# A four-layer decoder trunk on one core: a new opening, whole tiles from GpSimd, and another order at the norms and in the attention mixer

## The chip, the cores and the metric

The kernel runs on one core of a Trainium2 chip. The metric is the device time of one execution in microseconds (us). TensorE is called PE here (PEld is its weight load), VectorE DVE, ScalarE ACT, GpSimd POOL, and SyncE SP.

## The reference

Two layers (the depth of this case), each with a half-step SwiGLU feed-forward network (FFN), a token mixer and another half-step FFN; the mixer of layer 0 is an mLSTM (mixer A), that of layer 1 differential attention (mixer B). Sequence 512, model width 1024, FFN width 2816, all in fp32.

```python
for i in range(DEPTH):
    ada = (cond @ ada_w[i] + ada_b[i]).reshape(-1, 3, 3, D_MODEL)
    h = modulate(x, norm_g[i, 0], ada[:, 0, 0], ada[:, 0, 1])   # rmsnorm(x, g) * (1 + scale) + shift
    x = x + 0.5 * ada[:, 0, 2, None, :] * swiglu(h, ffn_w13[i, 0], ffn_w2[i, 0])
    h = modulate(x, norm_g[i, 1], ada[:, 1, 0], ada[:, 1, 1])
    y = mlstm_mixer(h, ...) if i % 2 == 0 else diff_attn_mixer(h, ...)
    x = x + ada[:, 1, 2, None, :] * y
    h = modulate(x, norm_g[i, 2], ada[:, 2, 0], ada[:, 2, 1])
    x = x + 0.5 * ada[:, 2, 2, None, :] * swiglu(h, ffn_w13[i, 1], ffn_w2[i, 1])
return rmsnorm(x, final_g)
```

## The kernel before, in words

**Data and products.** x is kept transposed, as 8 tiles (k = 0 to 7) of 128 features by 512 tokens. Each fp32 product is made of three matmuls of rounded parts, hi x hi, lo x hi and hi x lo (`three`, L710 to L712). Weights come in units of 128 x 1024, eight blocks of 128 x 128, one per k: SP loads a unit into one of two buffers (`load_unit`, L545; the load of unit u waits until the low part of unit u - 2 is made), ACT makes its high part (L1212), DVE its low part (L1707), and PE needs both. With 512 tokens a unit is 8 products, 24 matmuls. Each engine works through its own written list of instructions in order, and semaphores join them; so what stands behind a waiting instruction on its engine waits too.

**Norms.** Five norms stand between the six sublayers, and one at the end; n = 1, 3 and 4 follow an FFN, n = 2 and 5 a mixer. Each works in two halves of 256 tokens. Per k DVE makes the modulated tile (L1767), ACT the high part h_hi, with the shift as bias (L1220, the "split"), and DVE h_lo = tile + shift - h_hi (L1719, the "low"). For k = 2, 4 and 6 of half 0, ACT adds the shift to the tile in place (L1225) and POOL makes h_lo from it (L698), a "joint". Between these stand the high and low parts of the first units U to U + 3 of the next sublayer. PE's `first_group` begins on the tiles as they come: in half 0 units 0 and 1 side by side, k by k, then units 2 and 3; in half 1 units 0 to 2 side by side, then unit 3.

**FFN.** An FFN p (0 to 3; after norms 0, 2, 3 and 5) has 8 plain pairs of gate and up units in p = 0 and 4 in the others, then 14 or 18 fast pairs, which need fewer products, of sums of tiles. These sums (L1869 on DVE, split on ACT at L1283, and their low parts) are made from whole modulated tiles `mod`, the shift included; ACT makes them (`full_modulated`, L1275). The low parts of the first factors of weights (L1914) come behind them. The gate products are ACT's L1261 (from PSUM) and DVE's L1849, g_lo is L1854. Before the fast pairs SP writes x into DRAM (`store_x`, L571), since its space is used.

**Opening.** For FFN 0 the modulation vectors of norm 0 are made on DVE (L1812, one pass for scale and one for shift per k) from eight slices `early_ada` of 1 MB. For k = 4 to 7 POOL makes the shift's product (L693) and ACT sums it. Per k DVE makes the tile `mod` (L2446) and h_lo (L2451), and ACT columns of scale and shift and h_hi (L1658). ACT also keeps half of x's tiles (`keep_x`, L1635). POOL makes the low parts of units 0 to 3 (L685). PE's `opening_group` (L806) works on units 0 to 3, with matmuls on zeros (L821) put in: 8 before the first product and 24 between the products.

**Mixer B.** DVE's loop over passes n does, per pass: mask and maxima of the scores (L2304 to L2306), a rotation of one head's q or k (`rope`, L2293 to L2297), a low part and copies of head outputs. PE makes scores (L1096) and column sums (`head_sum`, L1132).

## Time and profile before

| | |
|---|---|
| time, median of 3 runs (lowest, highest) | 1906.97 us (1905.39, 1909.76) |
| the profiled execution: its time, its span | 1905.79 us, 1903.9 us |
| PE busy | 1867.1 us, 98% of the span |
| DVE, ACT, POOL busy | 1430.1 us (75%), 894.9 us (47%), 35.9 us (2%) |
| mean granted PE clock | 0.996 |
| chain that ended last | PE 82%, DVE 9%, ACT 3%, DMA 3%, issue 2% |
| DMA | 273.51 MB, mean 144 GB/s |

The span is that of one execution recorded by the profiler. A busy engine is one with an instruction in work. The granted clock is what the throttle allows PE, as a share of 2.4 GHz. A wait is idle time of an engine in front of an instruction, put down to the instruction that released it.

### The profile page before, as it was taken

Reading aid. Unit: us, or ns where it says so; the run is one execution under the profiler, and the core shown is the slowest. Engines: PE = TensorE matmul, PEld = TensorE weight load, DVE = VectorE, ACT = ScalarE, POOL = GpSimd, SP = SyncE. Lnnn points to the kernel's source line nnn. Section 1 sums busy time; section 2 is a strip of 40 time slices with the busy share of each in tenths; the row PEclk is TensorE's granted clock in tenths of the full one; section 3 lists DMA queues with packets and bytes.
Section 4 is the critical chain, followed back from the end, with each engine's and each line's share of the span. In section 5 each row is a group of like instructions: output and inputs, shape, how many; then the busy total and the mean of one; then the engine's idle time right before and its main releaser. Section 6 shows DMA issues by size and latency. Waiting matters only on the chain.

```text
span 1903.9 us, 30428 instructions
## 1 busy us (share of the span) xinstructions
PE 1867.1 (98%) x11752; PEld 1678.9 (88%) x11752; DVE 1430.1 (75%) x2000; ACT 894.9 (47%) x1435; POOL 35.9 (2%) x35
## 2 busy tenths in 40 slices
PE   7999999999999999999999999999999999999997
PEld 5799998888778999998899999889877799999886
DVE  6788868686577888868678888796786778888434
ACT  6266542244344656642265565224444456566321
POOL 4000000000000000000000000000000000000000
PEclk9999999999999999999999999999999999999999
DMA  8733259624213432349733322973321233323432
GB/s 345 265 111 111 100 183 338 240 89 155 66 56 101 133 111 90 109 179 334 260 122 122 110 89 86 344 254 89 111 67 45 67 124 121 109 90 105 135 98 82
DMA packets 86002, 273.51 MB, mean 144 GB/s; under 512 B 8560, under 2 KB 18928, under 8 KB 84888
## 3 DMA queue, kind: packets, MB, share of 16 engines
q1 hardware_dynamic: 85712, 271.83, 41.6%
q8 instruction: 51, 0.84, 0.2%
q10 hardware_dynamic: 200, 0.52, 0.1%
q14 instruction: 39, 0.32, 0.0%
HBM read 261.82 MB, written 10.50 MB: 143 GB/s over the span
## 4 chain that ended last, share of the span: by engine, by line
PE 82%; DVE 9%; ACT 3%; DMA 3%; issue 2%; SPq 0%; DVEq 0%; ACTq 0%
PE outp L711 12%; PE outp L712 12%; PE outp L710 12%; PE acc L710 11%; PE acc L712 11%; PE acc L711 11%; PE stats L710 2%; PE stats L712 2%; PE stats L711 2%; DVE w_lo L1707 2%; DMA arena<-w 1%; PE outp L1000 1%; DMA early_ada<-ada 1%; ACT w_hi L1212 1%; ACT mod L1275 1%
## 5 line engine op out<-in xcount | busy, mean ns | idle before, releaser
L710 PE MATMUL acc<-h_hi,w_hi 128*128 128x256 f32 (+1 forms) x1220 | 397.8, 326 | 11.1 <-DVE w_lo L1707 5.5
L1212 ACT ACTIVATE w_hi<-arena 128x1024 fp32r<-128x1024 f32 (+2 forms) x231 | 209.9, 909 | 383.4 <-DMA arena<-w 192.5
L711 PE MATMUL acc<-h_lo,w_hi 128*128 128x256 f32 (+1 forms) x1220 | 389.2, 319 | 0.0
L712 PE MATMUL acc<-h_hi,w_lo 128*128 128x256 f32 (+1 forms) x1220 | 389.1, 319 | 0.0
L1914 DVE TENSOR_TENSOR w_lo<-arena,w_hi 128x1024 fp32r<-128x1024 f32 (+1 forms) x272 | 290.5, 1089 | 101.7 <-ACT w_hi L1292 97.9
L1707 DVE TENSOR_TENSOR w_lo<-arena,w_hi 128x1024 fp32r<-128x1024 f32 (+2 forms) x229 | 236.6, 1035 | 165.6 <-ACT w_hi L1212 164.2
L1292 ACT ACTIVATE w_hi<-arena 128x1024 fp32r<-128x1024 f32 (+1 forms) x272 | 257.8, 949 | 75.8 <-PE stats L712 28.6
L710 PE MATMUL outp<-g_hi,w_hi 128*128 128x512 f32 (+1 forms) x792 | 290.2, 366 | 0.0
L711 PE MATMUL outp<-g_lo,w_hi 128*128 128x512 f32 (+1 forms) x792 | 289.5, 365 | 0.0
L712 PE MATMUL outp<-g_hi,w_lo 128*128 128x512 f32 (+1 forms) x792 | 289.4, 365 | 0.0
L710 PEld LDWEIGHTS acc<-h_hi,w_hi 128*128 128x128 f32 x1220 | 232.6, 191 | 34.8 <-issue 9.8
L711 PEld LDWEIGHTS acc<-h_lo,w_hi 128*128 128x128 f32 x1220 | 232.8, 191 | 17.3 <-issue 1.4
L712 PEld LDWEIGHTS acc<-h_hi,w_lo 128*128 128x128 f32 x1220 | 232.6, 191 | 16.5
L710 PEld LDWEIGHTS outp<-g_hi,w_hi 128*128 128x128 f32 x792 | 149.4, 189 | 24.4
L711 PEld LDWEIGHTS outp<-g_lo,w_hi 128*128 128x128 f32 x792 | 149.4, 189 | 24.3
L712 PEld LDWEIGHTS outp<-g_hi,w_lo 128*128 128x128 f32 x792 | 149.3, 189 | 23.7
L710 PE MATMUL acc<-t_hi,w_hi 128*128 128x256 f32 x544 | 154.0, 283 | 0.0
L711 PE MATMUL acc<-t_lo,w_hi 128*128 128x256 f32 x544 | 154.0, 283 | 0.0
L712 PE MATMUL acc<-t_hi,w_lo 128*128 128x256 f32 x544 | 154.0, 283 | 0.0
L710 PE MATMUL outp<-h_hi,w_hi 128*128 128x256 f32 x436 | 123.8, 284 | 0.0
L712 PE MATMUL outp<-h_hi,w_lo 128*128 128x256 f32 x436 | 123.4, 283 | 0.0
L711 PE MATMUL outp<-h_lo,w_hi 128*128 128x256 f32 x436 | 123.4, 283 | 0.0
(280 smaller groups left out, 3426.7 us busy)
## 6 DMA issues: line engine op xcount, KB each, us to landing
arena<-w SPq DMA_DIRECT2D x174, 512.0 KB, 3.7
ada_raw<-ada SPq DMA_DIRECT2D x64, 512.0 KB, 5.9
arena<-ada SPq DMA_DIRECT2D x56, 512.0 KB, 5.9
arena<-w SPq DMA_DIRECT2D x64, 384.0 KB, 3.6
arena<-w SPq DMA_DIRECT2D x64, 320.0 KB, 4.5
arena<-wa SPq DMA_DIRECT2D x33, 512.0 KB, 3.6
arena<-wb SPq DMA_DIRECT2D x32, 512.0 KB, 3.6
early_ada<-ada SPq DMA_DIRECT2D x8, 1024.0 KB, 17.7
```

Source lines behind the costliest of these rows:

```text
L710: pe.matmul(bank, a_hi, b_hi, start=start, stop=False, skip_group_check=onto)
L711: pe.matmul(bank, a_hi, b_lo, start=False, stop=False, skip_group_check=onto)
L712: return pe.matmul(bank, a_lo, b_hi, start=False, stop=stop, skip_group_check=onto)
L1000: last = pe.matmul(outp[:, d, j * P:S], a_v[:, j, c0:c0 + P], w, start=j == 0, stop=j == ST - 1)
L1212: act.activation(w_hi[base % SLOTS][:, 0:n], src[:, 0:n], ACT.Copy).then_inc(hi_ready, 1)
L1275: act.activation(mod[:, k, t], mod[:, k, t], ACT.Identity, bias=ada_v[:, 3 * N_FFN[p], k:k + 1]).then_inc(full_ready, 1)
L1292: act.activation(slot(w_hi[(B + n) % SLOTS], n), two_factors(j, n), ACT.Copy).then_inc(hi_ready, 1)
L1707: dve.tensor_tensor(w_lo[s][:, 0:n], raw[base % RAWS][:, 0:n], w_hi[s][:, 0:n].bitcast(F32), ALU.subtract).then_inc(lo_ready, 1)
L1914: dve.tensor_tensor(slot(w_lo[s], n), two_factors(j, n), slot(w_hi[s], n).bitcast(F32), ALU.subtract)\
```

## The change

- **Opening.** The modulated tile of each k goes to the PSUM bank `stat` instead of `mod`, one buffer for all k. DVE makes low(0) ahead of the passes of k = 1, and later each low between the scale pass and the shift pass of the next k. ACT makes the split of k = 0 before it keeps x tiles 6 and 7, and its high parts 1 to 3 stand at other places. PE's zero matmuls start when two x tiles are kept on ACT, go to bank 1, and are 8 + 12; the order of the products of k = 0 and 1 is another. SP writes x to DRAM behind the first early slices and before the load of unit 6. In FFN 0's first pair ACT's high part of unit 4 stands before the gate.
- **Norms.** There are no joints; DVE makes all h_lo. For n = 1, 3 and 4 ACT's high part of U + 2 stands behind the split of k = 0, for n = 2 and 5 behind that of k = 4; that of U + 3 stands behind all splits of half 0. For n = 2 and 5 DVE's low part of U + 1 stands before `add(4)`. In half 1 PE takes units 0 to 2 side by side for k < 6 alone, and then k = 6 and 7 unit by unit.
- **Whole tiles.** POOL makes them, as h_hi + h_lo (32 instructions of 512 columns, 8 per FFN); ACT's 32 are gone. In FFN 0 each follows its low, in the others all follow the last low of the norm.
- **Mixer B.** The rotations of passes 6 and 10 stand ahead of the maxima.

The places where the order of instructions changes, as lists of one engine. **ACT at the head of norm 1** (`w_hi_54` to `w_hi_57` hold the high parts of units U to U + 3). Before:

```order
L1229 ACTIVATE rstd<-stats,eps 128x256 [waits stat_done]
L1212 ACTIVATE w_hi_54<-arena 128x1024 [waits unit_done,raw_loaded0]
L1212 ACTIVATE w_hi_55<-arena 128x1024 [waits unit_done,raw_loaded1,ada_ready]
L1220 ACTIVATE h_hi<-mod,ada_v 128x256 [waits src_ready] x3
L1225 ACTIVATE mod<-mod,ada_v 128x256
L1220 ACTIVATE h_hi<-mod,ada_v 128x256 [waits src_ready] x2
L1225 ACTIVATE mod<-mod,ada_v 128x256
L1212 ACTIVATE w_hi_56<-arena 128x1024 [waits unit_done,raw_loaded0]
L1220 ACTIVATE h_hi<-mod,ada_v 128x256 [waits src_ready] x2
L1225 ACTIVATE mod<-mod,ada_v 128x256
L1212 ACTIVATE w_hi_57<-arena 128x1024 [waits unit_done,raw_loaded1]
L1220 ACTIVATE h_hi<-mod,ada_v 128x256 [waits src_ready]
```

And now, where line numbers are lower:

```order
L1225 ACTIVATE rstd<-stats,eps 128x256 [waits stat_done]
L1211 ACTIVATE w_hi_54<-arena 128x1024 [waits unit_done,raw_loaded0]
L1211 ACTIVATE w_hi_55<-arena 128x1024 [waits unit_done,raw_loaded1,ada_ready]
L1219 ACTIVATE h_hi<-mod,ada_v 128x256 [waits src_ready]
L1211 ACTIVATE w_hi_56<-arena 128x1024 [waits unit_done,raw_loaded0]
L1219 ACTIVATE h_hi<-mod,ada_v 128x256 [waits src_ready] x7
L1211 ACTIVATE w_hi_57<-arena 128x1024 [waits unit_done,raw_loaded1]
```

Unit U + 2 moved from behind the fifth split to behind the first, seven splits stand behind it, and the activations of `mod` are gone.

**DVE in the opening**, from the first tile on (`ISA` on early_ada is a pass). Before:

```order
L2446 SCALAR_TENSOR_TENSOR mod<-x,scale_col,stats 128x512 [waits rstd_spread,scale_made]
L1812 ISA early_ada,early_sum<-early_ada,outp 128x1024 [waits early_loaded1]
L1812 ISA early_sum 128x1
L1812 ISA early_ada,early_sum<-early_ada,outp 128x1024
L1812 ISA early_sum 128x1
L2451 SCALAR_TENSOR_TENSOR h_lo<-mod,ada_v,h_hi 128x512 [waits act_hi_ready]
L2446 SCALAR_TENSOR_TENSOR mod<-x,scale_col,stats 128x512 [waits scale_made]
```

And now:

```order
L2445 SCALAR_TENSOR_TENSOR stats<-x,scale_col,stats 128x512 [waits rstd_spread,scale_made]
L2450 SCALAR_TENSOR_TENSOR h_lo<-stats,ada_v,h_hi 128x512 [waits act_hi_ready]
L1805 ISA early_ada,early_sum<-early_ada,outp 128x1024 [waits early_loaded1]
L1805 ISA early_sum 128x1
L1805 ISA early_ada,early_sum<-early_ada,outp 128x1024
L1805 ISA early_sum 128x1
L2445 SCALAR_TENSOR_TENSOR stats<-x,scale_col,stats 128x512 [waits act_lo_ready,scale_made]
```

The low of k = 0 moved ahead of both passes of k = 1; each later tile waits for the low before it, since it has the same buffer.

**DVE in pass 6 of mixer B**, maxima and rotation. Before:

```order
L2304 TENSOR_TENSOR acc<-acc,mask_ts 128x2x128 [waits s_done]
L2305 TENSOR_REDUCE row_max<-acc 128x2 [waits dve_step]
L2306 TENSOR_SCALAR neg_max<-row_max 128x2 [waits dve_step]
L2293 STREAM_SHUFFLE b_rot<-b_qk 32x512 [waits acc_free0]
L2294 TENSOR_TENSOR b_tmp<-b_qk,b_cos 32x512 [waits dve_step]
L2296 TENSOR_TENSOR b_rot<-b_rot,b_sin 32x512
L2297 TENSOR_TENSOR b_qk<-b_tmp,b_rot 32x512 [waits dve_step]
L1707 TENSOR_TENSOR w_lo_61<-arena,w_hi_57 128x1024 [waits hi_ready,rope_done]
```

And now:

```order
L2286 STREAM_SHUFFLE b_rot<-b_qk 32x512 [waits acc_free0]
L2287 TENSOR_TENSOR b_tmp<-b_qk,b_cos 32x512 [waits dve_step]
L2289 TENSOR_TENSOR b_rot<-b_rot,b_sin 32x512
L2290 TENSOR_TENSOR b_qk<-b_tmp,b_rot 32x512 [waits dve_step]
L2297 TENSOR_TENSOR acc<-acc,mask_ts 128x2x128 [waits s_done,rope_done]
L2298 TENSOR_REDUCE row_max<-acc 128x2 [waits dve_step]
L2299 TENSOR_SCALAR neg_max<-row_max 128x2 [waits dve_step]
L1700 TENSOR_TENSOR w_lo_61<-arena,w_hi_57 128x1024 [waits hi_ready]
```

The four instructions of the rotation moved ahead of the three of the maxima.

The diff, without the lines in which `lows_made` becomes a plain wait:

```diff
@@ -142,11 +142,2 @@
 Q_IN = (Q_F0, Q_A, Q_F1, Q_F2, Q_B, Q_F3, Q_RESULT)
-POOL_LOWS = tuple(Q_IN[n] + k for n in range(1, SUBS) for k in (2, 4, 6))
-def pool_lows(i):
-    return sum(t < i for t in POOL_LOWS)
 HALVES = tuple(SQ_BASE[r] - KT * r for r in range(SUBS))
@@ -569,3 +551,7 @@
-                    sp.wait_ge(src_ready, Q_IN[n] + KT * (half + 1 if p else 1))
+                    if p:
+                        sp.wait_ge(src_ready, Q_IN[n] + KT * (half + 1))
+                    else:
+                        sp.wait_ge(x_kept_dve, 4)
+                        sp.wait_ge(x_kept_act, 4)
                     sp.dma_start(x_copy[:, :, tok(half)], x[:, :, tok(half)]).then_inc(x_stored, 16)
@@ -589,5 +575,5 @@
                                 load_ada(sl, k)
-                        if i == 0:
-                            store_x(0)
-                            store_x(1)
+                            if i == 0 and m == 1:
+                                store_x(0)
+                                store_x(1)
                     for m in range(2 * PLAIN[p] - 4, 2 * PLAIN[p]):
@@ -695,10 +681,14 @@
-            def joint_low(n, k):
-                pool.wait_ge(joint_full, pool_lows(Q_IN[n] + k + 1))
-                pool.tensor_tensor(h_lo[:, k, tok(0)], modulated_home(Q_IN[n], k)[:, tok(0)],
-                                   h_hi[:, k, tok(0)].bitcast(F32), ALU.subtract).then_inc(pool_lo_ready, 1)
-            for n in range(1, SUBS):
-                for k in (2, 4, 6):
-                    joint_low(n, k)
+            def whole(p, k):
+                pool.wait_ge(act_lo_ready, Q_IN[N_FFN[p]] + (2 * KT if p else k + 1))
+                pool.tensor_tensor(mod[:, k, :], h_hi[:, k, :].bitcast(F32), h_lo[:, k, :].bitcast(F32), ALU.add)\
+                    .then_inc(full_ready, 1)
+            for k in range(KT):
+                whole(0, k)
+            for p in range(1, 4):
+                for k in range(KT):
+                    whole(p, k)
@@ -741,4 +731,5 @@
                     together = 3 if half else 2
-                    for k in range(KT):
-                        lows_made(pe, Q_IN[n] + 8 * half + k + 1)
+                    side_by_side = KT - 2 if half else KT
+                    for k in range(side_by_side):
+                        pe.wait_ge(act_lo_ready, Q_IN[n] + 8 * half + k + 1)
                         for s in range(together):
@@ -747,2 +738,6 @@
                                 take_acc(T, s)
+                            product(s, k, half)
+                    for s in range(together):
+                        for k in range(side_by_side, KT):
+                            pe.wait_ge(act_lo_ready, Q_IN[n] + 8 * half + k + 1)
                             product(s, k, half)
@@ -824,9 +819,13 @@
                 pe.wait_ge(zero_ready, 1)
-                pe.wait_ge(x_kept_act, 4)
-                add_zeros(3, 8, alone=True)
-                for pair in range(2):
-                    for k in range(2):
-                        for s in (2 * pair, 2 * pair + 1):
-                            product(s, k)
-                        add_zeros(2 * pair, 4)
+                pe.wait_ge(x_kept_act, 2)
+                add_zeros(1, 8, alone=True)
+                product(0, 0)
+                product(1, 0)
+                add_zeros(0, 6)
+                product(2, 0)
+                add_zeros(0, 3)
+                for s in range(3):
+                    product(s, 1)
+                for k in range(2):
+                    product(3, k)
                 for k in range(2, KT):
@@ -834,4 +833,4 @@
                         product(s, k)
-                    if k < 4:
-                        add_zeros(0, 4)
+                    if k == 2:
+                        add_zeros(0, 3)
@@ -1222,5 +1221,2 @@
                 ins.then_inc(act_hi_ready, 1)
-                if q in POOL_LOWS:
-                    home = modulated_home(q - k, k)[:, t]
-                    act.activation(home, home, ACT.Identity, bias=bias[:, k:k + 1]).then_inc(joint_full, 1)
@@ -1239,6 +1235,7 @@
                     split_high(Q_IN[n] + k, k, tok(0), ada_v[:, 3 * n, :])
-                    if k in (4, 6):
-                        high_part(U + k // 2)
+                    if k == (4 if mixer else 0):
+                        high_part(U + 2)
                     if mixer and k in LATE_MIXER:
                         last_square(4 + LATE_MIXER.index(k))
+                high_part(U + 3)
                 if not mixer:
@@ -1269,9 +1266,2 @@
                 B, W, F, c = U_FAST[p], W_FFN[p], FAST_BEFORE[p], PLAIN[p] - 4
-                def full_modulated(ks):
-                    for k in ks:
-                        lows_made(act, Q_IN[N_FFN[p]] + (KT if p else 0) + k + 1)
-                        t = tok(1) if Q_IN[N_FFN[p]] + k in POOL_LOWS else slice(0, S)
-                        act.activation(mod[:, k, t], mod[:, k, t], ACT.Identity,
-                                       bias=ada_v[:, 3 * N_FFN[p], k:k + 1]).then_inc(full_ready, 1)
@@ -1320,3 +1310,2 @@
                 product_high(p, c)
-                full_modulated(range(KT // 2))
                 gate_of(p, c + 1)
@@ -1324,3 +1313,2 @@
                 product_high(p, c + 1)
-                full_modulated(range(KT // 2, KT))
                 high_part(U + 7)
@@ -1362,4 +1350,8 @@
                     u = U_FFN[p] + 2 * f
-                    gate_of(p, f)
-                    high_part(u + 4)
+                    if f:
+                        gate_of(p, f)
+                        high_part(u + 4)
+                    else:
+                        high_part(u + 4)
+                        gate_of(p, f)
                     product_high(p, f)
@@ -1657,3 +1649,3 @@
                 act.wait_ge(shift_made, k + 1)
-                act.activation(h_hi[:, k, :], mod[:, k, :], ACT.Identity, bias=ada_v[:, 0, k:k + 1])\
+                act.activation(h_hi[:, k, :], stat[:, :], ACT.Identity, bias=ada_v[:, 0, k:k + 1])\
                    .then_inc(act_hi_ready, 1)
@@ -1666,13 +1658,14 @@
             scale_column(0)
+            high_part(1)
             shift_column(0)
+            first_split(0)
             keep_x(6)
             keep_x(7)
-            high_part(1)
-            for k in range(KT):
+            high_part(2)
+            for k in range(1, KT):
+                scale_column(k)
+                shift_column(k)
                 first_split(k)
-                if k + 1 < KT:
-                    scale_column(k + 1)
-                    shift_column(k + 1)
-                if k < 2:
-                    high_part(k + 2)
+                if k == 1:
+                    high_part(3)
             norm(1, U_A, ffn(0))
@@ -1748,2 +1741,3 @@
                     if k == 4:
+                        low_part(U + 1)
                         add(4)
@@ -1752,3 +1746,2 @@
                         add(5)
-                        low_part(U + 1)
                     if k == 6:
@@ -2372,2 +2365,4 @@
                         low_part(U + 25)
+                    if n in (6, 10):
+                        rope(4 + n)
                     maxima(n)
@@ -2377,3 +2372,3 @@
                         low_part(U + 12 + n)
-                    if n < 12:
+                    if n < 12 and n not in (6, 10):
                         rope(4 + n)
@@ -2433,5 +2428,7 @@
-            def first_tiles(k):
+            def first_scale(k):
                 dve.wait_ge(early_loaded[k], 16)
                 ada_tile(early_ada[:, k, 1, :], cond_bank, early_sum[:, 1, k:k + 1], scale_summed)
+            def first_shift(k):
                 if k not in POOL_SHIFTS:
@@ -2445,3 +2442,5 @@
                     dve.wait_ge(x_kept_act, k - 3)
-                dve.scalar_tensor_tensor(out=mod[:, k, :], in0=x[:, k, :], scalar=scale_col[:, k:k + 1],
+                if k:
+                    dve.wait_ge(act_lo_ready, k)
+                dve.scalar_tensor_tensor(out=stat[:, :], in0=x[:, k, :], scalar=scale_col[:, k:k + 1],
                                          in1=aux[:, :], op0=ALU.mult, op1=ALU.mult).then_inc(src_ready, 1)
@@ -2450,3 +2449,3 @@
                 dve.wait_ge(act_hi_ready, k + 1)
-                dve.scalar_tensor_tensor(out=h_lo[:, k, :], in0=mod[:, k, :], scalar=ada_v[:, 0, k:k + 1],
+                dve.scalar_tensor_tensor(out=h_lo[:, k, :], in0=stat[:, :], scalar=ada_v[:, 0, k:k + 1],
                                          in1=h_hi[:, k, :].bitcast(F32), op0=ALU.add, op1=ALU.subtract)\
@@ -2454,8 +2453,15 @@
-            first_tiles(0)
-            for k in range(KT):
+            first_scale(0)
+            first_shift(0)
+            first_modulated(0)
+            first_low(0)
+            first_scale(1)
+            first_shift(1)
+            for k in range(1, KT):
                 first_modulated(k)
                 if k + 1 < KT:
-                    first_tiles(k + 1)
+                    first_scale(k + 1)
                 first_low(k)
+                if k + 1 < KT:
+                    first_shift(k + 1)
             for j in range(2):
```

## Rows read from the trace of the kernel before

**Rows 1.** Waits of PE over the whole span, by what ended them.
```profile
PE acc L710 <- DVE w_lo L1707: 5.5, 10, 2.3
...
PE acc L710 <- DVE h_lo L1719: 2.1, 2, 1.1
...
PE stats L1132 <- DVE b_qk L2332: 1.4, 2, 1.0
...
PE acc L1096 <- DVE b_qk L2297: 0.7, 1, 0.7
...
PE acc L710 <- ACT b_qk L1519: 0.5, 1, 0.5
```

**Rows 2.** Timeline of PE, opening: start, us, engine, operation [idle before <-releaser].
```profile
23.04 0.47 PE L710 MATMUL acc<-h_hi,w_hi 128*128 128x512 f32 x1 [0.33 <-DVE h_lo L2451]
...
52.96 0.47 PE L710 MATMUL acc<-h_hi,w_hi 128*128 128x512 f32 x1 [1.03 <-DVE w_lo L1707]
...
77.32 0.76 PE L710 MATMUL acc<-h_hi,w_hi 128*128 128x512 f32 x1 [2.32 <-DVE w_lo L1707]
```

**Rows 3.** After unit 8's start: us; busy PE, PEld, DVE, ACT, POOL; clock; DMA share; GB/s.
```profile
77.30:80.00 2.70, 2.68 (x6) 2.14 (x7) 2.70 (x5) 0.00 (x0) 0.00 (x0) 0.50 1.02 408
80.00:82.00 2.00, 2.00 (x9) 1.63 (x8) 1.04 (x3) 1.90 (x3) 0.00 (x0) 0.83 1.05 418
```

**Rows 4.** Timeline of DVE and POOL in the opening.
```profile
21.22 1.68 DVE L2451 SCALAR_TENSOR_TENSOR h_lo<-mod,ada_v,h_hi 128x512 fp32r<-128x512 f32 x1
...
43.24 0.75 DVE L2451 SCALAR_TENSOR_TENSOR h_lo<-mod,ada_v,h_hi 128x512 fp32r<-128x512 f32 x1 [1.15 <-ACT h_hi L1658]
...
19.97 2.38 POOL L685 TENSOR_TENSOR w_lo<-arena,w_hi 128x1024 fp32r<-128x1024 f32 x1 [2.39 <-ACT w_hi L1212]
```

**Rows 5.** DVE's passes (ns min/median/max); DMA issue at 64.3 (KB, us to landing).
```profile
L1812 DVE CUSTOM_DVE_ANT_0 early_ada<-early_ada,outp x12: 1205/1210/1221, 15.3 to 39.2; 128x1024 f32<-128x1024 f32 x12
...
arena<-w SPq DMA_DIRECT2D x1, 512.0 KB, 10.5
```

**Rows 6.** Head of norm 1: PE, SP's load, ACT, and the busy time there.
```profile
386.08 0.36 PE L710 MATMUL acc<-h_hi,w_hi 128*128 128x256 f32 x1
...
392.96 0.39 PE L710 MATMUL acc<-h_hi,w_hi 128*128 128x256 f32 x1 [0.16 <-DVE w_lo L1707]
...
382.92 0.33 SPq L545 DMA_DIRECT2D arena<-wa  x1
...
arena<-wa SPq DMA_DIRECT2D x1, 512.0 KB, 3.5
...
387.66 1.04 ACT L1212 ACTIVATE w_hi<-arena 128x1024 fp32r<-128x1024 f32 x1
...
386.00:393.00 7.00, 6.12 (x46) 5.34 (x44) 5.37 (x11) 5.25 (x11) 2.34 (x3) 1.00 0.27 75
```

**Rows 7.** Timeline of PE at the head of norm 2.
```profile
616.56 0.39 PE L710 MATMUL acc<-h_hi,w_hi 128*128 128x256 f32 x1 [0.96 <-DVE h_lo L1719]
```

**Rows 8.** Timeline of PE, first unit after norm 1's group.
```profile
411.79 0.47 PE L710 MATMUL acc<-h_hi,w_hi 128*128 128x512 f32 x1 [0.89 <-DVE w_lo L1707]
```

**Rows 9.** POOL's joints; then DVE, PEld and busy time in FFN 1.
```profile
L698 POOL TENSOR_TENSOR h_lo<-mod,h_hi x15: 737/756/1435, 386.6 to 1545.2; 128x256 fp32r<-128x256 f32 x15
...
628.64 0.48 DVE L1719 SCALAR_TENSOR_TENSOR h_lo<-mod,ada_v,h_hi 128x256 fp32r<-128x256 f32 x1 [0.18 <-ACT h_hi L1220]
...
643.41 1.23 DVE L1869 TENSOR_TENSOR mod<-mod 128x1024 f32<-128x1024 f32 x1 [0.99 <-ACT mod L1275]
...
657.57 0.19 PEld L873 LDWEIGHTS outp<-h_hi,w_hi 128*128 128x128 f32 x1 [0.56 <-DVE w_lo L1914]
...
629.50:643.40 13.90, 13.90 (x87) 12.55 (x86) 7.30 (x8) 10.77 (x17) 0.00 (x0) 1.00 0.50 155
```

**Rows 10.** Timeline of DVE in mixer B.
```profile
1410.57 0.43 DVE L2304 TENSOR_TENSOR acc<-acc,mask_ts 128x256 f32<-128x256 f32 x1 [4.56 <-PE acc L1096]
```

17 lines of the change are left out of this document (5 added, 12 removed).

## The prediction

> **What bounds the kernel now.** I read first the totals by engine and the waits of PE. PE is busy 98% of the span, so that nearly all time is matmul work which the change leaves alone, apart from twelve zero matmuls, and what can be won is PE's idle time and its slow clock. The waits of PE that the change touches are few: 5.5 us on low parts of weights, 2.1 us on the h_lo of the norms, 1.4 us and 0.7 us in the attention mixer, 0.5 us on a copy of ACT [rows 1]. A line sums what lies far apart, so I went to the timeline next. In the opening the first product starts at 23.04, unit 4 at 52.96 after a pause of 1.03, and unit 8 at 77.32 after one of 2.32 [rows 2]. Behind that last pause PE has half its clock (granted 0.50, that is 1.2 of 2.4 GHz) for 2.70 us and 0.83 for two more: 2.70 x 0.50 + 2.00 x 0.17 = 1.7 us of work lost on top of the gap [rows 3]. The remaining pauses are at the heads of the five norms and in mixer B; they are taken below with their places. After unit 8 no pause is above 1.5 us, so the whole change works on some 20 us.
>
> **The opening (gain 5.9).** Three things set when unit 4 starts: when the first h_lo is made, how much work PE has, and when the last h_lo is made. Before, DVE made scale and shift of k=1 ahead of the low of k=0, so that low(0) ran from 21.22 for 1.68 us [rows 4]. Now low(0) comes directly behind the modulated tile, without the two passes of k=1 (1.21 each [rows 5]) and, reading PSUM, at 0.75 and not 1.68: 2.4 + 0.9 less, so that it ends at about 19.7 instead of 22.9. For that ACT splits h_hi(0) before it keeps x tiles 6 and 7. PE's work from there is 32 products of 0.69 (unit 4 to unit 8, 32 products and 2.32 of pause, are 24.4 us [rows 2]) and 12 zero matmuls of a third of that, where 24 stood: 22.1 + 2.8 = 24.9 us. With 1.4 us for waits on k=1 and k=2, an estimate, unit 3 ends near 46.0 instead of 51.9. The supply must follow: the loads of the slices and POOL's products are as before, when the last low ran from 43.24 for 0.75 [rows 4], so k=7 is there at 44.0 at the latest. PE comes to it at 46.0 - 4 x 0.69 = 43.3, so this costs at most 0.7; I put it at 0, since DVE has less to do ahead of it. The pause before unit 4 stays at about 1: the activation of w_hi(4) now stands before the first gate on ACT, and its table load behind it. Unit 4 at 47.05 instead of 52.96: -5.9. The two ends: with the supply as the bound and a pause of 2, -4; with the supply early and no pause, -7.
>
> **Unit 8 (gain 4.0).** Its weights were loaded behind the two x_copy stores and under a full DMA share (1.02); a load issued there took 10.5 us to land [rows 3, 5]. The stores now go out before the load of unit 6. They need x alone, which is complete then. SP's order behind them is the same, so the load of unit 8 has nothing before it but slices. But it starts with PE 5.9 us earlier, and each load waits for a low part, so the whole queue moves with PE. The 2.32 gap and the half clock go: -2.3 - 1.7 = -4.0, ends 0 (the loads of units 6 and 7 inherit the delay) and -4.0. Opening and unit 8 together: -9.9.
>
> **The norms 1, 3 and 4 (loss 6.0).** Here the order of ACT changes most. high_part(U+2) stood at k=4, now it stands behind split 0, and ACT's splits 1 to 7 are queued behind it. At norm 1 its load is issued at 382.92 and takes 3.5 to land, at 386.4 [rows 6]. ACT needs 1.0 for it (387.4, [rows 6]), then split 1 and DVE's low 1 come, 0.45 each: 388.3. PE came to k=1 at 386.08 before, so it now stands for 2.3 us; a gap of that size is just what was followed by the half clock at 77.32 [rows 3, 6]. The lows then come every 0.8 us, as DVE makes the modulated tile and the low in turn (0.48 each in [rows 9], overlapping by 0.08), so k=7 is there at 393.2, and the third unit starts at 394.3 at full clock and 395.35 at half, where it started at 392.96 [rows 6]. The stall is thus partly paid with idle time that exists already: PE was busy 6.12 of 7.00 us there [rows 6]. That is +1.35 to +2.4; I take 2.0 for each, nearer to the half clock, since that row has the same gap. Three times: +6.0. The three copies of ACT (L1225) and three joints of POOL that go away per norm save nothing more here, since the wait now stands ahead of them; the 3 lows of 0.40 that DVE gets are in the pace of 0.8.
>
> **The norms 2 and 5 (gain 3.2).** These keep high_part(U+2) behind split 4. The last k tile of the first pair of units waits 0.96 for its h_lo at 616.56, and norm 5 has the other wait of the 2.1 us [rows 1, 7]. Of the 5.5 us on w_lo, 5.5 - 1.03 - 2.32 - 0.89 = 1.3 is left for seven waits at the five heads; three are the 0.16 of norms 1, 3 and 4, and four with 0.8 together lie here [rows 1, 2, 6, 8]. Of what DVE does ahead of that h_lo, low_part(U+1) and an update change places, high_part(U+2) and the splits of ACT are free of the three copies, and nothing waits for POOL's joints of 0.76 [rows 9]. I take 1.0 + 0.4 for the waits and 0.2 for slower matmuls behind them, 1.6 each; ends 0.8 and 2.
>
> **Half 1 by unit (gain 1.2).** PE now finishes unit 0 of the first group earlier by the last two k tiles less of two other units: two products of 0.36 [rows 6], 0.72 us. The work is the same; the slot is free for high and low part of the next unit 0.72 earlier. After norm 1 the wait is 0.89 at 411.79 [rows 8]: -0.7. After norm 4, in mixer B, it is 0.5, on ACT [rows 1]: -0.5. Ends 0 and -1.6.
>
> **Whole tiles (loss 3.0).** ACT made them; now POOL does, 8 instructions per FFN. The trace has no POOL instruction of this form with 512 columns. From below: half of the 2.38 of w_lo with 1024 columns, 1.19. From above: twice the 0.74 of the joints with 256, 1.48 [rows 4, 9]. I take 1.19, since a fixed part is counted twice in the upper one. Its start is after the last low of the norm. In FFN 1, half 1 of the norm begins at T = 623.7 (the 616.56 of [rows 7], 18 products of 0.36, and 0.65 for the norm's sum and short waits), and its last low, at 628.64, ends at 629.1, T + 5.5 [rows 9]. 8 x 1.19 = 9.5 would end at T + 15.0 and hurt nobody, since the first sum over all tiles (L1869) starts at 643.41, T + 19.7 [rows 9]. But in the opening the low with three SBUF operands took 1.68 while POOL was at work, and the same operation has 0.75 at 43.24 when POOL is idle [rows 4]: the two engines kept each other off. DVE has 7.30 us of work in these 13.9 [rows 9], of which all but the two gate products (L1849, one operand in PSUM, 0.75 each like the row at 43.24) have two operands in SBUF: 5.8. If all of it excludes POOL, the tiles are done at T + 5.5 + 9.5 + 5.8 = T + 20.8, 1.1 later than now. DVE's sums, ACT's t_hi and the first factors' w_lo follow in one chain, and PE's weight load waits 0.56 at the end of it already [rows 9], so a delay goes through: +1.0 each in FFN 1, 2 and 3, +3.0. Ends: no exclusion, -0.4 each; POOL at 1.48 each, +3.4 each. In FFN 0 the tiles are made one by one in the opening, as POOL is between its shift products; nothing.
>
> The Trainium skill (SBUF — State Buffer, section "Who interferes with whom") says that a DVE operation with two SBUF inputs and a GpSimd operation that reads SBUF hold a shared port pair as an exclusive lock, for the whole instruction. The trace agrees with 1.68 against 0.75. By that rule the w_lo, g_lo and sums are exactly the ones which block; it speaks against this part of the change. The page GPSIMD Engine Reference (section 3.1, Elementwise) has 4497 ns for a tensor_tensor add of 2048 columns; an estimate from it is 1.12 us for 512, with which the sum would be 0.6 less per FFN.
>
> **Rotations (gain 1.4).** In mixer B, DVE waited 4.56 us for PE's scores before the maxima of one pass, with the rotation queued behind them [rows 10]. Two rotations now go into that idle time. What waited for it: head_sum 1.0 of the 1.4 us, and the scores 0.7 [rows 1]. I take 0.7 + 0.7; ends 0 and 2. The idle 4.56 hides the four instructions of a rotation; without it the maxima, and the scores' successors, would be late by them.
>
> **Sum.** -5.9 - 4.0 + 6.0 - 3.2 - 1.2 + 3.0 - 1.4 = -6.7. The profiled execution took 1905.79 (span 1903.9), so 1899.1; it is 1.2 below the median of the runs, 1906.97, so 1900.3 against that.
>
> **Rivals.** (A) POOL and DVE don't block each other for these forms: the 1.68 could have come from something else, as it is one instruction. Whole tiles -0.4 x 3 instead of +3.0: 1896.1. (B) The stall at high_part(U+2) doesn't occur: its load lands before split 0 is done. Against it is the 3.5 us of the landing row; for it that SP's order may put the load earlier when low_part(U) is early. Then the +6.0 goes, and 0.5 of the 0.88 that PE is idle there [rows 6], three times: 1892.8. (C) The opening and unit 8 gain only half of the 9.9: the single bank makes tile, split and low follow one another, so that lows come later than PE needs them, or the stores delay the loads of units 6 and 7 and the pause merely moves. Nothing in the rows excludes either. +4.95: 1905.2. (D) Slower: ACT is held at high_part(U+2) of norms 1, 3 and 4 by loads that land late. It decides when the three stalls cost more than (6.7 + 3.8)/3 + 2.0 = 5.5 us each, that is, when the landing takes 3.5 us longer than the 3.5 seen; at 4 us longer the time is 1900.3 + 12 = 1912.3. For it: a landing of 10.5 under a full DMA share [rows 5]. Against: the share was 0.27 there [rows 6].
>
> **How the numbers follow.** A measurement of this kernel can tell 0.2%, 3.8 us, from no change. Forecast 0.60, A 0.11, B 0.10, C 0.14, D 0.05. Forecast, A and B lie below 1903.2, but for 0.02 of the forecast that its unknown terms (POOL's price above all) put over it: faster 0.79. C and that rest are within 0.2%: 0.16. D is slower: 0.05. The forecast's own bounds, -3 on the opening and norms and +4 on the whole tiles, give 1896 to 1904; with A wholly and part of C the range is 1894.0 to 1905.5. B lies below it, D above.
>
> **What would show it.** Right: unit 4 near 47; no pause and no clock of 0.5 at unit 8; a new pause of about 2 on PE at k=1 of norms 1, 3 and 4, released by a DVE h_lo whose h_hi waited for ACT's w_hi; L1869's successor starting 1 us later against half 1; POOL's tiles 1.2 long but spread over 15 us. Wrong: no pause at the three norms (B), or pauses of over 5 (D); POOL's tiles back to back and DVE's w_lo still 1.15 beside them (A); a pause of 2 or more at any of units 4 to 8 (C).

## The result, and the profile after

The changed kernel takes 1896.48 us (median of 5 runs, 1895.55 to 1897.19), the kernel before 1905.39 (5 runs, 1903.75 to 1909.76): ratio 0.9944, 95% interval 0.9932 to 0.9955. The forecast was 1900.3 against 1907.0, a gain of 6.7 us; the measured one is 8.9 us between the medians. The changed kernel's profiled execution took 1897.00 us, 8.8 less than the 1905.79 of the one before, and its span is 1894.9 against 1903.9.

PE's row of the page: the busy time fell by 5.8 us, of which 2.8 are the 12 zero matmuls (0.23 each).

```profile
PE 1861.3 (98%) x11740; PEld 1678.6 (89%) x11740; DVE 1442.2 (76%) x2015; ACT 873.7 (46%) x1388; POOL 72.9 (4%) x52
```

PE's waits in the changed kernel (in total, times, longest). These answer to [rows 1]: the wait for low parts of weights fell from 5.5 to 1.3, the one for h_lo rose from 2.1 to 6.8, three pauses instead of two, and there is a new row, 3.3 us at the start of the fast pairs. The wait of head_sum fell from 1.4 to 0.5.

```profile
PE acc L700 <- DVE h_lo L1712: 6.8, 3, 2.4
...
PE outp L872 <- DVE w_lo L1907: 3.3, 3, 1.3
...
PE acc L700 <- DVE w_lo L1700: 1.3, 2, 1.2
```

The kernel before had one more row, which is gone: 0.7 us at each of the norms 1, 3 and 4 for POOL's h_lo.

```profile
PE acc L710 <- POOL h_lo L698: 2.1, 6, 0.5
```

In the timeline of PE the same is seen with its places. It answers to [rows 2]; there is no row at unit 8 any more.

```profile
19.73 0.47 PE L700 MATMUL acc<-h_hi,w_hi 128*128 128x512 f32 x1 [1.35 <-DVE h_lo L2450]
...
47.44 0.47 PE L700 MATMUL acc<-h_hi,w_hi 128*128 128x512 f32 x1 [1.18 <-DVE w_lo L1700]
...
378.74 0.39 PE L700 MATMUL acc<-h_hi,w_hi 128*128 128x256 f32 x1 [2.18 <-DVE h_lo L1712]
...
648.00 0.38 PE L872 MATMUL outp<-h_hi,w_hi 128*128 128x256 f32 x1 [1.34 <-DVE w_lo L1907]
...
954.36 0.39 PE L700 MATMUL acc<-h_hi,w_hi 128*128 128x256 f32 x1 [2.21 <-DVE h_lo L1712]
...
1307.38 0.39 PE L700 MATMUL acc<-h_hi,w_hi 128*128 128x256 f32 x1 [2.39 <-DVE h_lo L1712]
```

The windows of the changed kernel (us; busy us of PE, PEld, DVE, ACT, POOL; granted clock, DMA share, GB/s): unit 8's start, the head of norm 1, and the plain pairs of FFN 1, to be set beside [rows 3, 6, 9]. Half the clock has left unit 8 and has come to norm 1 (0.79 and 0.59 in the two windows behind the pause).

```profile
68.00:72.00 4.00, 4.00 (x19) 3.34 (x18) 3.30 (x7) 0.98 (x2) 0.00 (x0) 1.00 0.98 370
...
378.70:381.00 2.30, 2.26 (x14) 2.24 (x15) 2.30 (x7) 1.32 (x3) 0.00 (x0) 0.79 0.00 0
381.00:384.00 3.00, 3.00 (x19) 3.00 (x17) 2.82 (x7) 2.18 (x4) 0.00 (x0) 0.59 0.00 0
...
618.40:632.50 14.10, 14.10 (x90) 12.75 (x89) 10.13 (x7) 7.09 (x9) 13.45 (x8) 1.00 0.46 150
```

From the third k tile of the opening on, both kernels have the same matmuls in the same order but for the zeros and the end of the norms' half 1, so each matmul of the one can be set beside the same of the other, counted from the end; the difference of the starts changes only where time is won or lost. These are the steps between the two profiled executions, against the terms of the sum:

| place | forecast | measured |
|---|---|---|
| opening, to unit 4 | -5.9 | -5.5 |
| unit 8, pause and half clock | -4.0 | -4.2 |
| heads of norms 1, 3, 4 | +6.0 | +2.05 +1.26 +2.29 = +5.6 |
| heads of norms 2, 5 | -3.2 | -2.1 -2.0 = -4.1 |
| first unit behind norms 1, 4 | -1.2 | -0.72 -0.84 = -1.6 |
| whole tiles, FFN 1, 2, 3 | +3.0 | +1.20 +0.84 +0.84 = +2.9 |
| rotations | -1.4 | -0.69 -0.75 -0.16 = -1.6 |
| smaller steps | 0 | -0.5 |
| sum | -6.7 | -9.0 |

### The profile page after: what moved, and what is told of

The parts are those of the page before. It is cut to its first block, busy times and chain, and to the rows that moved or that the text cites. A ratio compares the mean times of both kernels' runs of the same rounds, so it can differ in the third digit from the quotient of the medians.

```text
span 1894.9 us, 30209 instructions
## 1 busy us (share of the span) xinstructions
PE 1861.3 (98%) x11740; PEld 1678.6 (89%) x11740; DVE 1442.2 (76%) x2015; ACT 873.7 (46%) x1388; POOL 72.9 (4%) x52
## 4 chain that ended last, share of the span: by engine, by line
PE 87%; DVE 8%; DMA 2%; ACT 1%; issue 1%; SPq 0%; POOL 0%; DVEq 0%; ACTq 0%
PE outp L700 13%; PE outp L701 13%; PE outp L702 13%; PE acc L700 12%; PE acc L702 12%; PE acc L701 12%; PE stats L700 2%; PE stats L702 2%; PE stats L701 2%; DVE w_lo L1700 2%; DMA raw<-w 1%; DVE mod L1862 1%; PE outp L999 1%; PE acc L1095 1%; DMA arena<-wa 1%
## 5 line engine op out<-in xcount | busy, mean ns | idle before, releaser
L1700 DVE TENSOR_TENSOR w_lo<-arena,w_hi 128x1024 fp32r<-128x1024 f32 (+2 forms) x229 | 243.5, 1065 | 153.8 <-ACT w_hi L1211 152.1
```

Source lines behind the costliest of these rows:

```text
L1700: dve.tensor_tensor(w_lo[s][:, 0:n], raw[base % RAWS][:, 0:n], w_hi[s][:, 0:n].bitcast(F32), ALU.subtract).then_inc(lo_ready, 1)
```

## The experiments

Twelve experiments stand below, each on the changed kernel unless something else is said. Experiments 1 and 12 were executed four times, the others once. Where one execution was taken, the difference is read from the steps of its trace, since the kernel before spreads over 8 us from run to run. Two kinds of steps come and go whatever the edit is: up to 0.9 us at unit 8, and 0.6 to 1.0 us at the head of one of the norms 1, 3 and 4, as half the clock follows the pause there or doesn't. So a step below 1 us counts here only where its place shows a wait that belongs to the edit.

**1. The high part of U + 2 back.** In ACT's `norm`:

```diff
-                    if k == (4 if mixer else 0):
+                    if k == 4:
                         high_part(U + 2)
```

> The changed kernel with ACT's high part of unit U+2 behind the split of k=4 again at norms 1, 3 and 4 (where it stood before), all else as changed. Theory (ACT held at that high part by its load): the pauses of 2.2 to 2.4 us at k=1 and the half clock behind two of them go; the three heads cost 5.6 us more in the changed kernel than before, so at least 5.6 goes: 1890.9 against 1896.5, and up to 1 us more, since POOL's joints, for which PE waited 0.7 us per head before, are gone too. Rival (the pauses come from the missing joints: DVE makes eight lows instead of five and is late): the pauses stay, within 1 us of 1896.5.

Measured: 1889.43 us (1889.20 to 1889.52, 4 runs), ratio to the kernel before 0.9908 (0.9891 to 0.9924); 7.05 below the changed kernel. The steps are -2.8, -2.0 and -3.0 at norms 1, 3 and 4, and at most 0.4 elsewhere. PE's wait for h_lo and the window that answers to [rows 6]:

```profile
PE acc L700 <- DVE h_lo L1712: 0.7, 3, 0.2
...
376.00:383.00 7.00, 6.65 (x50) 6.15 (x50) 6.48 (x15) 4.74 (x8) 0.00 (x0) 1.00 0.29 94
```

0.7 us is left of 6.8, and PE is busy 6.65 of 7.00 us. The theory holds, and the edit was a loss. The steps sum to 7.8, which is 2.2 more than the 5.6 that the three heads had cost: without the joints the waits of 2.1 us for POOL's h_lo stay away too (experiment 8 finds 0.4 per head for the joints alone; the rest isn't put down to one edit). How the loss came about stands in the changed kernel's rows, SP, DMA, ACT and DVE at norm 1. SP's row has two loads, of U + 2 at 373.25 and of U + 3; the landing is that of the first.

```profile
373.25 1.85 SPq L527 DMA_DIRECT2D arena<-wa  x2
...
arena<-wa SPq DMA_DIRECT2D x1, 512.0 KB, 3.4
...
376.71 1.06 ACT L1211 ACTIVATE w_hi<-arena 128x1024 fp32r<-128x1024 f32 x1 [2.56 <-DMA arena<-wa]
...
378.20 0.48 DVE L1712 SCALAR_TENSOR_TENSOR h_lo<-mod,ada_v,h_hi 128x256 fp32r<-128x256 f32 x1 [2.27 <-ACT h_hi L1219]
```

The load lands near 376.65 (373.25 + 3.4), and ACT, which stood 2.56 us for it, begins at 376.71; DVE's low, 2.27 us idle, had to wait for the split behind it.

**2. The whole tiles back on ACT.** `full_modulated` is ACT's again for p = 1 to 3:

```diff
+                def full_modulated(ks):
+                    for k in ks if p else ():
+                        act.wait_ge(act_lo_ready, Q_IN[N_FFN[p]] + KT + k + 1)
+                        act.activation(mod[:, k, :], mod[:, k, :], ACT.Identity,
+                                       bias=ada_v[:, 3 * N_FFN[p], k:k + 1]).then_inc(full_ready, 1)
...
-            for p in range(1, 4):
-                for k in range(KT):
-                    whole(p, k)
```

> The changed kernel with the whole tiles of FFN 1, 2 and 3 made by ACT again (eight activations of 512 columns each, at the places they had), FFN 0's still by POOL. Theory (POOL's tiles and DVE's two-operand instructions exclude each other): DVE's w_lo beside them are back at 1.2 us each (1.55 to 2.19 in the changed kernel), the waits of 1.3 us for L1907 at the start of each FFN's fast pairs shrink to the 0.3 to 0.6 of before, -2.9 us in all: 1893.6. Rival (the delay comes from elsewhere, the new order of ACT's list): no change.

Measured: steps of -0.91, -0.93 and -0.92 at the three places, 1893.58 us. In the changed kernel, POOL's eight tiles and DVE's instructions with two SBUF inputs beside them look so:

```profile
618.43 13.45 POOL L685 TENSOR_TENSOR mod<-h_hi,h_lo 128x512 f32<-128x512 f32 x8 [567.04 <-DVE h_lo L1712]
...
621.75 1.55 DVE L1700 TENSOR_TENSOR w_lo<-arena,w_hi 128x1024 fp32r<-128x1024 f32 x1 [3.40 <-ACT w_hi L1211]
624.61 2.19 DVE L1700 TENSOR_TENSOR w_lo<-arena,w_hi 128x1024 fp32r<-128x1024 f32 x1 [0.19 <-ACT w_hi L1211]
626.72 1.78 DVE L1847 TENSOR_TENSOR g_lo<-buf,g_hi 128x512 fp32r<-128x512 f32 x1
628.43 2.31 DVE L1862 TENSOR_TENSOR mod<-mod 128x1024 f32<-128x1024 f32 x1
...
631.26 1.71 DVE L1700 TENSOR_TENSOR w_lo<-arena,w_hi 128x1024 fp32r<-128x1024 f32 x1
632.89 0.68 DVE L1847 TENSOR_TENSOR g_lo<-buf,g_hi 128x512 fp32r<-128x512 f32 x1
633.50 1.21 DVE L1862 TENSOR_TENSOR mod<-mod 128x1024 f32<-128x1024 f32 x1
```

And with the tiles on ACT, the second w_lo of DVE, and PE's wait for the first factors:

```profile
624.75 1.22 DVE L1705 TENSOR_TENSOR w_lo<-arena,w_hi 128x1024 fp32r<-128x1024 f32 x1 [0.19 <-ACT w_hi L1208]
...
PE outp L869 <- DVE w_lo L1912: 0.4, 1, 0.4
```

The same instruction takes 1.22 us and not 2.19, and the wait of 3.3 is 0.4. (In this execution half the clock did not follow the pause at norm 4, -0.8; +0.3 stands against it in the opening.) POOL's side shows the exclusion too: eight tiles of 1.28 are 10.3 us of work and took 13.45. But the last tile is ready at 631.88, and the sum L1862 starts at 633.50 straight behind DVE's own g_lo, with no wait for a tile. What is late is DVE's list, of which five instructions are stretched by 4 us in all: with the tiles on ACT the same five take 1.23, 1.22, 0.68, 1.23 and 1.22.

**3. The whole tiles shared.** ACT makes k = 0 to 3, POOL k = 4 to 7, on a semaphore of its own:

```diff
-                    dve.wait_ge(full_ready, KT * p + (KT if i else KT // 2))
+                    dve.wait_ge(full_ready, KT + KT // 2 * p if p else (KT if i else KT // 2))
+                    if p and i:
+                        dve.wait_ge(full_pool, KT // 2 * p)
```

> The changed kernel with the whole tiles of FFN 1, 2 and 3 shared out: k = 0 to 3 by ACT, k = 4 to 7 by POOL at the same time. Theory (mutual exclusion, 8 x 1.28 us of POOL and 5.8 of DVE add up): with 4 tiles the sum is 5.1 + 5.8 and ends 5 us before the sums need it, and ACT carries half of its old load: -2.9 to -3.8 us, 1893 or a little under. Rival (each single w_lo that is stretched delays the chain, however many tiles): about half goes, -1.4.

Measured: -1.60, -1.24 and -1.24, 4.1 us in the FFNs, 1892.0 us in one execution (a further 0.9 is clock at norm 4). Slightly over the theory's range of 2.9 to 3.8, and far from the rival's 1.4. The trace has one instruction of DVE still stretched, the first w_lo (1.55), since POOL is done with its four tiles before the next; that is 0.3 us of stretching in place of 4. The theory's reason, the readiness of the last tile, isn't the one: it is DVE's list, as said above.

**4. The stores of x back.**

```diff
-                            if i == 0 and m == 1:
-                                store_x(0)
-                                store_x(1)
+                        if i == 0:
+                            store_x(0)
+                            store_x(1)
```

> The changed kernel with the two stores of x in FFN 0 back at their old place on SP's queue, between the load of unit 7 with its two slices and the load of unit 8. Theory (the place of the stores makes unit 8 late): a pause of about 2.3 us before unit 8 and half the clock for 3.4 us behind it return, +4.1 us: 1900.6. Rival (the pause went because of the new opening): no change. If PE, which now comes to unit 8 earlier by 5.5 us, finds the queue even less ready, the pause is longer than 2.3.

Measured: 1905.25 us, with a step of +7.6 at unit 8. PE, SP, the load issued at 60.66 (KB, us to landing) and the window behind the pause:

```profile
74.23 0.77 PE L700 MATMUL acc<-h_hi,w_hi 128*128 128x512 f32 x1 [4.68 <-DVE w_lo L1700]
...
58.56 2.05 SPq L557 DMA_DIRECT2D x_copy<-x  x2
60.66 4.36 SPq L527 DMA_DIRECT2D arena<-w  x1
...
arena<-w SPq DMA_DIRECT2D x1, 512.0 KB, 11.1
...
74.20:80.00 5.80, 5.77 (x14) 4.59 (x15) 4.85 (x8) 2.66 (x4) 0.00 (x0) 0.53 1.02 402
```

The load of unit 8 waits on SP's queue behind the stores and then needs 11.1 us to land. So the pause is 4.68 and not 2.3, with 6.8 us at half clock. The third case of the expectation came: PE is 5.5 us earlier at units 4 to 7, but without this move the queue isn't, and 7.6 of the 9.7 us won by then are lost. In the changed kernel the stores hold SP's queue longer, 11.21 us and not 2.05, but at a time when its next load isn't due before 47.32:

```profile
29.97 11.21 SPq L557 DMA_DIRECT2D x_copy<-x  x2
47.32 0.33 SPq L527 DMA_DIRECT2D arena<-w  x1
```

**5. The opening's tile in SBUF.** `stat[:, :]` is `mod[:, k, :]` in L1650, L2445 and L2450.

> The changed kernel with the opening's modulated tile in SBUF (the tile mod, one place per k) instead of the PSUM bank; orders unchanged. Theory (a DVE instruction with two SBUF inputs and a POOL instruction exclude each other, one with a PSUM input does not take part): the lows L2450 of 0.75 us become 1.0 to 2.5 us wherever POOL works, POOL's instructions wait in turn, unit 4 starts 1 to 3 us later than 47.4 and the time rises by that: 1898 to 1900. Rival (the 1.68 us of the kernel before had another cause): lows at 0.75, no change.

Measured: 1901.12 us, 1.1 above the expected range, with unit 4 at 50.94 instead of 47.44: +3.5, where 1 to 3 was expected. PE is 1.1 us late at its first product and 0.8 at 29.5 us, and the other 2.7 come behind, from the low that starts at 31.86 on (a pause of PE of 1.19 at 34.49, and one of 0.59 at 38.14). Half the clock for 3.41 us also followed the pause of 2.64 before the first product, but the waits that the changed kernel has at 23.56 and 27.42 take most of that up. POOL, and three of DVE's lows:

```profile
17.75 2.35 POOL L671 TENSOR_TENSOR w_lo<-arena,w_hi 128x1024 fp32r<-128x1024 f32 x1 [0.38 <-ACT w_hi L1211]
21.07 2.38 POOL L671 TENSOR_TENSOR w_lo<-raw,w_hi 128x1024 fp32r<-128x1024 f32 x1 [0.96 <-ACT w_hi L1211]
25.38 2.41 POOL L671 TENSOR_TENSOR w_lo<-raw,w_hi 128x1024 fp32r<-128x1024 f32 x1 [1.93 <-ACT w_hi L1211]
29.01 4.88 POOL L679 TENSOR_TENSOR early_ada<-early_ada,cond 128x1024 f32<-128x1024 f32 x2 [1.22 <-DMA early_ada<-ada]
...
18.81 1.84 DVE L2450 SCALAR_TENSOR_TENSOR h_lo<-mod,ada_v,h_hi 128x512 fp32r<-128x512 f32 x1 [0.79 <-ACT h_hi L1650]
24.65 0.74 DVE L2450 SCALAR_TENSOR_TENSOR h_lo<-mod,ada_v,h_hi 128x512 fp32r<-128x512 f32 x1
...
31.86 2.57 DVE L2450 SCALAR_TENSOR_TENSOR h_lo<-mod,ada_v,h_hi 128x512 fp32r<-128x512 f32 x1
```

The first starts at 18.81 while POOL is at work until 20.10, and ends at 20.65; the third starts at 31.86, POOL ends at 33.89, and it ends at 34.43. The middle one has POOL idle and takes 0.74. Both long ones end 0.55 behind POOL's instruction, and so do four more that meet one (0.88 to 1.71 us long). In the changed kernel all eight, with the tile in PSUM and POOL as busy as here, are alike:

```profile
L2450 DVE SCALAR_TENSOR_TENSOR h_lo<-stats,ada_v,h_hi x8: 746/750/754, 18.8 to 42.3; 128x512 fp32r<-128x512 f32 x8
```

**6. The rotations back** (`rope(4 + n)` behind the maxima for all n).

> The changed kernel with the rotations of passes 6 and 10 behind the maxima again. Theory (they are in DVE's idle time before the maxima, and were late before): the waits for head_sum and for the scores return, +1.6 us, all of it between the passes 6 and 12 of mixer B: 1898.1. Rival (the gain there came with the other changes): no change.

Measured: waits return where they were, +2.35 and +0.77, 1900.13 us.

```profile
1418.84 0.27 PE L1131 MATMUL stats<-ones,b_qk 128*128 128x1 f32 x1 [1.04 <-DVE b_qk L2325]
...
1454.39 0.38 PE L1095 MATMUL acc<-b_qk 128*128 128x128 f32 x1 [0.69 <-DVE b_qk L2290]
```

Half the clock for 3.41 us followed the first wait this time. The step has +0.8 at the wait itself, near the 0.72 that this place gave in the change, and +1.6 behind it, which is what is above the 1.6 expected.

**7. Half 1 side by side again** (`side_by_side = KT`).

> The changed kernel with the first group's half 1 as before: units 0 to 2 side by side for all eight k. Theory (unit 0 is done two products of 0.36 later, and its slot is what the next unit waits for): +0.7 behind norm 1, +0.8 behind norm 4, nothing behind the others: +1.5: 1898.0. Rival (those waits went because ACT has fewer instructions at the norms now): no change.

Measured: +0.72 behind norm 1 and +0.74 behind norm 4, as PE's rows show (0.89 was there before, [rows 8]; behind norm 4 the wait is 0.41, on ACT); 1898.77 us with 0.8 more at unit 8, which isn't at this place.

```profile
404.54 0.47 PE L700 MATMUL acc<-h_hi,w_hi 128*128 128x512 f32 x1 [0.89 <-DVE w_lo L1700]
```

**8. The kernel before without joints** (`POOL_LOWS = ()`, and no `joint_low` calls).

> The kernel before, without POOL's joints and ACT's copies for them alone: DVE makes all h_lo. Theory (the joints cost more than they carry): at norms 1, 3 and 4 the 0.7 us of waits for POOL's h_lo go, and at norms 2 and 5 the wait of 0.96 to 1.1 for a DVE h_lo goes, together with some of the 0.4 for w_lo: -0.7 each for three and -1.5 each for two, -5 in all: 1902.4 against 1907.2. Rival (the gain at norms 2 and 5 is from the place of DVE's low part of U+1): at norms 2 and 5 less than 0.5 goes.

Measured: 1910.11 us, and the theory falls. At norms 1, 3 and 4 it is -0.4 each, and ACT's copies of whole tiles grew from half to full size, which costs some +0.6 in each FFN: the joints' end alone is worth nothing. At norms 2 and 5 only -0.2 to -0.4 goes. Nearly 4 us of the rest are pause and half clock at unit 8 and in mixer B. PE and ACT at norm 2:

```profile
617.94 0.39 PE L707 MATMUL acc<-h_hi,w_hi 128*128 128x256 f32 x1 [0.88 <-DVE h_lo L1716]
...
615.61 1.06 ACT L1209 ACTIVATE w_hi<-arena 128x1024 fp32r<-128x1024 f32 x1 [1.40 <-DMA arena<-w]
```

The wait for h_lo is still 0.88. Its cause is ACT's high part of unit U + 3, standing 1.40 for its load ahead of the split of k=7, which follows at 616.88. The kernel before has the same, and SP's row shows why: the second of two loads, that of U + 3, is issued at the end of 5.45 us, behind a low part.

```profile
614.23 1.06 ACT L1212 ACTIVATE w_hi<-arena 128x1024 fp32r<-128x1024 f32 x1 [1.01 <-DMA arena<-w]
...
605.52 5.45 SPq L545 DMA_DIRECT2D arena<-w  x2
```

In the changed kernel the same two are out after 3.44:

```profile
596.64 3.44 SPq L527 DMA_DIRECT2D arena<-w  x2
```

**9. DVE's low part of U + 1 back behind add(5)** (norms 2 and 5).

> The changed kernel with DVE's low part of U+1 behind add(5) again at norms 2 and 5. Theory (the joints' end gave the 2 us there): less than 0.5 us comes back. Rival (the place of this low part gave them): +1 us and more at each of the two heads, +2 to +4 in all.

Measured: 1897.88 us, +0.12 at norm 2 and +0.11 at norm 5. So it isn't this either, alone. SP's two loads are late as in the kernel before, out after 5.30 us, but no split of half 0 stands behind ACT's high part of U + 3:

```profile
597.05 5.30 SPq L527 DMA_DIRECT2D arena<-w  x2
```

**10. ACT's high part of U + 3 back ahead of the split of k=7.**

```diff
+                    if k == 6:
+                        high_part(U + 3)
                     if mixer and k in LATE_MIXER:
...
-                high_part(U + 3)
```

> The changed kernel with ACT's high part of unit U+3 ahead of the split of k=7 again, as before, at all five norms. The two runs on the joints and on DVE's low part of U+1 each explain at most 0.4 of the 2 us won per head at norms 2 and 5. New theory: this place won them, since in the kernel before ACT waited 1.01 us for the load of U+3 at 613.2 and made it (1.06) with the split of k=7, and so its h_lo, queued behind. Then +1.5 to +2 us at each of the norms 2 and 5: +3 to +4, 1900, with a wait for h_lo of about 1 us on PE at k=7. Rival (only all three edits together win it): less than +0.5 each. At norms 1, 3 and 4, where ACT comes to it later, neither expects more than 0.5.

Measured: 1897.63 us, +0.15 at norm 2 and +0.18 at norm 5. The new theory falls too, taken alone. Here the loads are out after 3.44 us, and ACT, ahead of the split of k=7, doesn't wait for one:

```profile
603.35 1.04 ACT L1211 ACTIVATE w_hi<-arena 128x1024 fp32r<-128x1024 f32 x1
```

The three runs and these rows fit one account: without either edit (experiment 8) the 2 us are missing, and with either one (9 has the moved high part, 10 the early low part) they are there. The load of U + 3 waits until the low part of U + 1 is made; made early, the load lands before ACT comes to it, and with the high part behind the split nobody queues behind the wait. Both edits mend one stall, and the second gives no more. (Two things weren't tried: the changed kernel with both edits undone, for which experiment 8 stands in, though it differs in more; and either edit with the joints in place.)

**11. No zeros between the products** (three `add_zeros` calls fewer, 12 matmuls).

> The changed kernel without the 12 zero matmuls between the opening's products (the 8 before them stay). Theory (they are work of 12 x 0.23 us in the way of PE): part of them fills waits for h_lo that exist anyway, so -0.5 to -2.8 us. Rival (they keep PE's clock up): the waits in the opening become pauses of 1.5 us and more, half the clock follows, 3.4 us at 1.2 GHz cost 1.7: no gain or up to 2 us slower.

Measured: 1898.00 us, with unit 4 at 47.22 instead of 47.44, though the first product came 0.3 late, at 20.01. Most of what the time is above the changed kernel's is a step of 1.0 at 1525 us, which isn't at this place.

```profile
23.81 0.50 PE L700 MATMUL acc<-h_hi,w_hi 128*128 128x512 f32 x1 [2.16 <-POOL w_lo L671]
...
47.22 0.50 PE L700 MATMUL acc<-h_hi,w_hi 128*128 128x512 f32 x1 [1.08 <-ACT buf L1254]
```

From the first product to unit 4 PE takes 27.2 us instead of 27.7, so of the zeros' 2.8 us some 0.5 is won. Most of the rest turned into waits for POOL's low parts of units 2 and 3: 2.16 and 0.55 where they were 0.84 and 0.17. In its first part the opening is bound by this supply as much as by PE, and behind the first h_lo the changed kernel's PE doesn't wait for one there. The rival's clock did not fall either, neither behind the 2.16 nor in the rest of the opening. The 0.5 is at the theory's low end and within what comes and goes from one execution to the next.

**12. Both mends together** (experiments 1 and 3).

> The changed kernel with both mends: the high part of unit U+2 back behind the split of k=4 at norms 1, 3 and 4 (alone -7.1 us against the changed kernel) and the whole tiles shared between ACT (k = 0 to 3) and POOL (k = 4 to 7) (alone -4.1 us of steps in the FFNs). They touch different places, so they add up: 1896.5 - 7.1 - 4.1 = 1885.3. If one of them uses time that the other had freed, 1887 or more.

Measured: 1885.53 us (1885.12 to 1885.87, 4 runs), ratio to the kernel before 0.9892 (0.9875 to 0.9908). The steps against the changed kernel are -2.8, -2.0 and -3.0 at the norms and -1.6, -1.2 and -1.2 in the FFNs: they add up. This version beats both kernels, the changed one by 10.95 us.

## Why the prediction was right

By its own steps:

- **Opening.** Right within 0.4 (unit 4 at 47.44, forecast 47.05). The first product came at 19.73, forecast 19.7, and from there to the end of unit 3 PE took 26.5 us, forecast 24.9 + 1.4. The reason given was half of it: the text took the last h_lo as the supply that could bind. What binds beside PE is POOL's low parts of units 2 and 3, which it did not price; without 2.8 us of zeros only 0.5 is won (experiment 11). The effect of PSUM on the low, 0.75 for 1.68, was right (experiment 5).
- **Unit 8.** Right in its mechanism and size (-4.2 for -4.0). But the sum counted it as a term beside the opening's, and it is a condition of that: without it the opening's gain is given back (experiment 4). Rival C had priced this as half of 9.9; it would have been 7.6.
- **Norms 1, 3 and 4.** Right: pauses of 2.18, 2.21 and 2.39 against the 2.3 worked out. Half the clock followed two of the three, so the steps are 2.05, 1.26 and 2.29; the 1.26 answers to the 1.35 worked out for full clock. The working of that 1.35 has a gap: from the last low at 393.2 two products of 0.36 lead to 393.9, not to the 394.3 in the text. In the trace PE doesn't wait for the lows at norm 3 once it has stood: the step is the late restart, 2.4, less 1.1 us of waits and short gaps that were there before, of which 0.7 were for POOL's h_lo. That the term came so near is partly luck, as which heads get half the clock changes from one execution to the next; over the ten traces with these pauses it followed 16 of 30.
- **Norms 2 and 5.** Right in sign, short by 0.9, and wrong in its reason: the text named the low part of U + 1 as work in front of an h_lo, and the end of ACT's copies. It did not see that ACT stood for the load of U + 3 ahead of the last split; it had the places in the order but no price. Experiments 8 to 10 give the cause: the low part of U + 1 matters because it releases that load, and the new place of the high part of U + 3 would have been enough too.
- **Whole tiles.** +2.9 for +3.0. Mutual exclusion is shown by experiments 2 and 5. The size came out, the way there didn't: the step "the tiles are done at T + 20.8" failed. POOL's tile is 1.28 us and not 1.19, the tiles were done at T + 19.0 (T is the start of the norm's half 1, here 612.9), and the sum started at T + 20.6 because DVE's own list was late.
- **Half 1 and rotations.** Right, each 0.2 to 0.4 more than forecast (experiments 6 and 7).

Between the traces the gain is 9.0 us, 2.3 above the forecast, and the measured time lies within the range given. The largest part of this is the term of norms 2 and 5 (0.9), then 0.4 each from half 1 and from the heads of norms 1, 3 and 4 and 0.5 of steps too small to have been listed, 0.5 more from unit 8, the tiles and the rotations together, while the opening gave 0.4 less. The seven terms were near enough that the result wasn't luck of one large one; but two of the edits are losses (+5.6 and +2.9) inside a change that gains, and that is what the prediction had said beforehand from the profile.

## What to carry to other kernels

When a step that waits for a load is moved forward in an engine's list, price everything queued behind it: here one activation moved ahead of seven short ones cost 2 to 3 us at each of three places (experiment 1), while its own consumer was in no hurry. An edit that makes a stage faster is worth only what the next load's place in the queue allows; look where the queue stands at the earlier time. And where two edits could mend the same stall, undoing one shows nothing; undo both, or start from a kernel that has neither.
